# A decoder step on one core: the normalised h gets a buffer of its own before the split u is remade

## The reference, cut to what matters

```python
def _rms(x, g):
    x32 = x.astype(jnp.float32)
    y = x32 * lax.rsqrt(jnp.mean(x32 * x32, axis=-1, keepdims=True) + RMS_EPS)
    return (y * g.astype(jnp.float32)).astype(x.dtype)

def _half_ffn(h, g_pre, g_post, w_gate, w_up, w_down):
    u = _rms(h, g_pre)
    f = (jax.nn.silu(u @ w_gate) * (u @ w_up)) @ w_down
    return h + 0.5 * _rms(f, g_post)
...
        hp = _half_ffn(hp, *ffn1)
        qa, ka, va, qb, kb, vb, ga, gb = _split_in(_rms(hp, g_mix_pre[layer]), w_in[layer])
        oa, ob, bufs, pages = _prompt_mixer(qa, ka, va, qb, kb, vb, b_sb[layer])
        hp = _merge(hp, oa, ob, ga, gb, *out_w)
        hp = _half_ffn(hp, *ffn2)
```

## Time and profile before

| | |
|---|---|
| median of 3 runs | 1298.46 us (1297.64 to 1300.94) |
| the profiled execution, its own time | 1299.87 us |
| its span, first to last instruction | 1298.1 us |
| TensorE matmul busy | 1248.8 us, 96% |
| VectorE, ScalarE, GpSimd busy | 504.9, 409.7, 505.4 us |
| mean granted TensorE clock | 0.986 of full speed |

### The profile page before, as it was taken

The page is one execution under the profiler, slowest core; times in us unless marked ns, Lnnn a source line. Parts: engine busy times, 40 slices in busy tenths (PEclk is TensorE's granted clock), DMA queues, the critical chain, the costliest instruction groups (busy, mean ns, idle before and its releaser), DMA issues.

```text
span 1298.1 us, 24918 instructions
## 1 busy us (share of the span) xinstructions
PE 1248.8 (96%) x10504; PEld 1214.1 (94%) x10504; DVE 504.9 (39%) x921; ACT 409.7 (32%) x678; POOL 505.4 (39%) x415
## 2 busy tenths in 40 slices
PE   8989999999999999999999889999989999999996
PEld 7989999999998989999988779999989999999995
DVE  4572322321116450355467411838572322321115
ACT  6232222212224242344445322335232222212220
POOL 1334444444454334322322513372234444444441
PEclk9999999999999989999999989999989999999998
DMA  6122222222213223302221376131122222222211
GB/s 231 43 89 80 82 97 97 97 88 91 90 65 123 80 86 115 103 34 99 82 83 67 117 224 196 66 130 39 66 91 79 85 97 97 97 86 93 90 58 66
DMA packets 29075, 123.26 MB, mean 95 GB/s; under 512 B 4442, under 2 KB 10610, under 8 KB 17394
## 3 DMA queue, kind: packets, MB, share of 16 engines
q1 hardware_dynamic: 28994, 122.09, 27.1%
HBM read 115.39 MB, written 6.67 MB: 94 GB/s over the span
## 4 chain that ended last, share of the span: by engine, by line
PE 84%; DVE 8%; DVEq 2%; DMA 2%; ACT 2%; issue 1%; SPq 1%; POOL 1%; POOLq 0%; ACTq 0%
PE bank L1420 25%; PE bank L1421 25%; PE bank L1422 25%; DVEq L1056 2%; PE bank L1442 2%; DVE f L1082 1%; PE bank L1611 1%; DVE u_lo L1073 1%; PE bank L1668 1%; PE bank L1653 1%; PE bank L1691 1%; PE bank L1640 1%; PE bank L1677 1%; DVE rinv L1062 1%; POOL w_lo L578 1%
## 5 line engine op out<-in xcount | busy, mean ns | idle before, releaser
L578 POOL TENSOR_TENSOR w_lo<-raw,w_hi 128x512 fp32r<-128x512 f32 x368 | 477.2, 1329 | 753.3 <-ACT w_hi L653 567.1
L1420 PE MATMUL bank<-u_hi,w_hi 128*128 128x260 f32 x1952 | 564.8, 289 | 15.8 <-DVE u_lo L1073 10.5
L1421 PE MATMUL bank<-u_lo,w_hi 128*128 128x260 f32 x1952 | 554.8, 284 | 0.0
L1422 PE MATMUL bank<-u_hi,w_lo 128*128 128x260 f32 x1952 | 554.7, 284 | 0.0
L1420 PEld LDWEIGHTS bank<-u_hi,w_hi 128*128 128x128 f32 x1952 | 371.2, 190 | 29.1 <-issue 17.1
L1421 PEld LDWEIGHTS bank<-u_lo,w_hi 128*128 128x128 f32 x1952 | 371.8, 190 | 0.0
L1422 PEld LDWEIGHTS bank<-u_hi,w_lo 128*128 128x128 f32 x1952 | 371.6, 190 | 0.0
L653 ACT ACTIVATE w_hi<-raw 128x2048 fp32r<-128x2048 f32 x81 | 154.8, 1911 | 304.4 <-PE bank L1422 304.4
L1420 PE MATMUL bank<-hid_hi,w_hi 128*128 128x260 f32 x704 | 199.4, 283 | 1.0 <-POOL w_lo L578 1.0
L1421 PE MATMUL bank<-hid_lo,w_hi 128*128 128x260 f32 x704 | 198.9, 283 | 0.0
L1422 PE MATMUL bank<-hid_hi,w_lo 128*128 128x260 f32 x704 | 198.8, 282 | 0.0
(11 more groups left out here) (192 smaller groups left out, 1304.7 us busy)
## 6 DMA issues: line engine op xcount, KB each, us to landing
raw<-w_stream SPq DMA_DIRECT2D x84, 1024.0 KB, 4.8
raw<-w_stream SPq DMA_DIRECT2D x8, 768.0 KB, 4.3
e_raw<-w_stream SPq DMA_DIRECT2D x5, 1024.0 KB, 8.6
h<-x_t SPq DMA_DIRECT2D x4, 520.0 KB, 7.1
y_t<-h SPq DMA_DIRECT2D x8, 260.0 KB, 2.3
block<-kb_pool SPq DMA_DIRECT2D x8, 256.0 KB, 3.5
ring<-kb_pool SPq DMA_DIRECT2D x8, 256.0 KB, 3.1
ring<-vb_pool SPq DMA_DIRECT2D x8, 256.0 KB, 4.7
```

What stands on the lines that cost most here:

```text
L578: return pool.tensor_tensor(low[:, a], src[:, a], top[:, a].bitcast(F32), ALU.subtract)
L1420: pe.matmul(out, w, hi_x, start=first, stop=False)
L1421: pe.matmul(out, w, lo_x, start=False, stop=False)
L1422: return pe.matmul(out, v, hi_x, start=False, stop=last)
```

## The change

Three buffers hn of the size of h are added, in memory that is free at the time: hn[0] and hn[2] where the FFN's low hidden values come later, hn[1] where the values of the mixer's attention come later. VectorE writes h times rinv there (normed) during chunk 2, behind that group's items of chunk 2, and not after chunk 3. The remaking proper keeps the rounding and the low part. The wait for the old u to be used up passes from VectorE to ScalarE. On ScalarE the high part of chunk 5 comes behind the u_hi of both groups, and on VectorE one more item (up_scale of bank 1) comes ahead of the first group's low parts. The drains between the steps are gone.

```diff
+    hn = [Placed(nc, R + (0 if q == 1 else 74880))(f"hn{q}", [P, KD, T]) for q in range(3)]
...
-            def u_top_again(q, g):
+            def u_top_again(q, g, r):
+
+                act.wait_ge(hn_made, 8 * q + 4 * g + 4)
+                act.wait_ge(full[2 * g + 1], r)
                 for t in range(KD):
-                    if t % 2 == 0:
-                        act.wait_ge(hn_made, 8 * q + 4 * g + t // 2 + 1)
-                    act.activation(u_hi[:, t, tg(g)], f[:, t, tg(g)], ACT.Copy,
+                    act.activation(u_hi[:, t, tg(g)], hn[q][:, t, tg(g)], ACT.Copy,
                                    scale=gain[:, 2 * q, t:t + 1]).then_inc(uh_made, 1)
...
-                for c in range(2):
-                    hi(n0 + FOLD + c)
-                    u_top_again(q, c)
+                hi(n0 + FOLD)
+                for g in range(G):
+                    u_top_again(q, g, r0 + FOLD)
+                hi(n0 + FOLD + 1)
...
-                    dve.scalar_tensor_tensor(u_lo[:, t, at], (f if again else h)[:, t, at],
+                    dve.scalar_tensor_tensor(u_lo[:, t, at], (hn[q] if again else h)[:, t, at],
...
-            def u_again(q, g, r):
-
-                dve.wait_ge(full[2 * g + 1], r)
+            def normed(q, g):
                 for s in range(4):
                     part = (slice(None), slice(2 * s, 2 * s + 2), tg(g))
-                    dve.tensor_tensor(f[part], h[part], wide(g), ALU.mult).then_inc(hn_made, 1)
-                    if s:
-                        drain()
-                        u_low(q, g, s - 1, again=1)
-                drain()
-                u_low(q, g, 3, again=1)
+                    dve.tensor_tensor(hn[q][part], h[part], wide(g), ALU.mult).then_inc(hn_made, 1)
+
+            def u_again(q, g):
+                for s in range(4):
+                    u_low(q, g, s, again=1)
...
-                for b in range(4):
-                    gate_scale(1, b, r0)
+                for g in range(G):
+                    gate_scale(1, 2 * g, r0)
+                    gate_scale(1, 2 * g + 1, r0)
+                    normed(q, g)
                 up_scale(1, 0, r0)
                 up_gate(q, 1, 0)
-                u_again(q, 0, r0 + FOLD)
-                for b in range(1, 4):
+                up_scale(1, 1, r0)
+                u_again(q, 0)
+                for b in range(2, 4):
                     up_scale(1, b, r0)
-                u_again(q, 1, r0 + FOLD)
+                u_again(q, 1)
```

More of the change, by code:

```diff
@@ L901, in hi_part @@
                     split.then_inc(hi_made, 1)
-            for c in range(2):
-                hi(QKV + FOLD + c)
-                u_top_again(1, c)
+            hi(QKV + FOLD)
+            for g in range(G):
+                u_top_again(1, g, R_QKV + FOLD)
+            hi(QKV + FOLD + 1)
             for c in range(FOLD, 9):
@@ L1223, in _ @@
                     project_scale(c, 2 * g + 1)
-            for b in range(4):
-                project_scale(2, b)
+            for g in range(G):
+                project_scale(2, 2 * g)
+                project_scale(2, 2 * g + 1)
+                normed(1, g)
             project_scale(3, 0)
             project_scale(3, 1)
-            u_again(1, 0, R_QKV + FOLD)
+            u_again(1, 0)
             project_scale(3, 2)
             project_scale(3, 3)
-            u_again(1, 1, R_QKV + FOLD)
+            u_again(1, 1)
             def place_v(n):
```

## The result

| | before | changed |
|---|---|---|
| median | 1299.41 us (4 runs; 1298.46 of the 3 shown ahead) | 1279.22 us (1278.53 to 1281.35, 4 runs) |
| ratio, 95% interval | | 0.9849 [0.9835, 0.9864] |
| the profiled execution, its own time | 1299.87 us | 1279.07 us |
| span | 1298.1 us | 1277.1 us |
| TensorE matmul busy | 1248.8 us | 1237.4 us |

The kernel is 1.5% faster, 19.6 us (17.7 to 21.4); 19.3 were forecast.

What follows compares the result with a forecast made beforehand. TensorE, busy 96% of the span, bounds the kernel; time goes where it stops or runs slowly. Three remakings lose 22.9 us, less two new stops of 1.8: 19.3 gained, 1298.46 - 19.3 = 1279.2 us, range 1275 to 1286.

Steps and rivals of the forecast that it cites:

- The size of the loss: Bank 0 of chunk 3 to bank 0 of chunk 5: three remakings lose 8.2 + 8.2 + 6.5 = 22.9 us.
- the two new stops: TensorE before chunk 5, one in each FFN: 1.8 us each, taken off the 22.9 us gained.
- The multiplications for nothing in chunk 2: VectorE in chunk 2: four multiplications of 0.69 us per group fit into idle time, cost zero.
- 5.5 us a place: Multiplications in chunk 2: what they would cost at each place without the cover of VectorE's idle time.
- Second group on time: First FFN: the second group's low parts end at 69.7 us, TensorE wants the first at 71.4; the old stop goes.
- The longer stop: TensorE before chunk 5 in each FFN, behind chunk 3's hidden values: about 1.8 us instead of 0.82, bounds 0 and 2.9.
- 69.7 + 0.5 = 70.2: First FFN: VectorE's start on chunk 3's hidden values, about 70.2 us, after the second group's low parts end at 69.7.
- Rival 2: Before chunk 5 in the FFNs: VectorE stands through all four GpSimd instructions, 2.9 us a stop, 1281.4 us; chance 0.08.
- The low part of chunk 5: GpSimd in the first FFN: ready at 76.4 to 77.0 us, wanted at 77.2; just hidden, cost 0 (0 to 0.5).
- The rival of the clock: New stop before chunk 5 in the FFNs: the clock still falls there, 1.7 us each, 1282.6 us; chance 0.10.
- rival 3: The rival of the clock by its number: clock falls at the new stop, 1.7 us each, 1282.6 us; chance 0.10.
- rivals 4 and 6: FFNs before chunk 5: 4, nine stretched hidden-value instructions, 1291 us, chance 0.06; 6, slower by VectorE-GpSimd conflict, 1306, chance 0.02.

Runs made afterwards that it cites:

- e5: The kernel before, with the product in a buffer of its own and the wait for the old u moved to ScalarE, all orders kept: 1299.08 us, ratio 0.9992.
- e7: The kernel before, with ScalarE's SiLU of each bank waiting only for the hidden values up to that bank: 1296.42 us, ratio 0.9977.
- e1: The changed kernel, with the multiplications put back right before their group's low parts, behind the items of chunk 3: 1301.01 us, ratio 1.0011.
- e3: The changed kernel, with ScalarE's SiLU of each bank waiting only for chunk 3's hidden values up to that bank, not all four: 1274.65 us, ratio 0.9817.
- e4: The changed kernel, with GpSimd waiting for all hidden values of chunk 3 before the low part of chunk 5, both FFNs: 1281.90 us, ratio 0.9866.
- e2: The changed kernel with ScalarE's old order, the high part of chunk 5 between the u_hi of the two groups: 1284.04 us, ratio 0.9896.

## Why the prediction was right

*The size of the loss.* 22.9 us were read from the distances between chunk 3 and chunk 5. The change gave back 6.8, 6.8 and 6.5 in them, 20.1 of the 20.8 us between the two profiled executions. TensorE's waits for u_lo alone would have given 10.5. One reservation: the projection's 29.5 is from one execution; e5 and e7, which leave TensorE the same wait there, have 28.6. The difference is in the clock: from 473 to 481 us it is 0.57 on the mean in the profile of before, 0.79 in that of e5. So 0.9 us of the 22.9 belongs to that execution.

*The agreement.* That the median came out at 1279.22, forecast 1279.2, is in part luck. The median of before rose by 0.95 us with its fourth run, and the gain is 20.2 us by the medians, 19.6 by the ratio. In the sum the loss was 0.9 us too large and the two new stops together 0.8 us too large, which cancel.

*The multiplications for nothing in chunk 2.* Right, at 0.63 instead of 0.69 us; the delay of the first item of chunk 3 was nil in the FFNs and 0.1 in the projection. That the loss of the cover would cost "5.5 us a place" was too low: with ScalarE's new order it cost 8.1, 5.6 and 8.3 (e1).

*Second group on time.* Ready at 69.3, wanted from 71.2 on; forecast 69.7 and 71.4, in an execution that runs 0.3 us earlier.

*The longer stop.* Forecast 1.8 us a place, measured 24.4 - 23.0 = 1.4. (The forecast's own terms, 78.9 - 77.2, give 1.7.) Its mechanism is shown from both sides by e3 and e4. The size was off by the term "69.7 + 0.5 = 70.2": VectorE began the hidden values 4.0 us after the end of chunk 3, not 4.5. The gap of 0.5 us between the last low part and the first hidden value was misread; 78.26 + 1.87 = 80.13 and the next start at 80.22 give 0.09, and so does the changed kernel (66.01 + 3.31 = 69.32, then 69.41). The nine instructions themselves took 7.9, forecast 8.0; three were through before GpSimd started, not two, four were stretched as forecast, and two were clear of it. Rival 2 (GpSimd first each time) is out: four stretched instructions, not one of 5.5 us. Its upper bound was added up wrongly: 71.0 + 5.5 + 7 x 0.47 + 0.7 - 77.2 is 3.3 us, not 2.9, and its time 1282.2 instead of 1281.4, still inside the range.

*The low part of chunk 5.* Ready at 76.1 and wanted at 76.9; in e3, where it alone could stop TensorE, it did not.

*The rival of the clock.* It did not fall at this stop of 1.16 us (1.00 in the windows from 71 to 81). But in e4 it fell after one of 1.81, in both FFNs, and what the windows there lack of full clock adds up to 1.7 us each, the price that rival 3 had (and the clock's share in rivals 4 and 6): 0.43 x 4, from the clock of 0.57 over the 4 us from 77 to 81 in the earlier trace rows. So the mechanism of rival 3 exists, and the row of 1.60 us without a fall was a thin ground against it.

*What was missed.* ScalarE's order was costed at nothing, as a delay that fits into slack. It is a gain of 5 to 6 us (e2): the high part of chunk 5 behind both groups holds GpSimd back from VectorE until the low parts of u are written, and the second group is rounded sooner. Counted from bank 0 of chunk 3, the hidden values start 5.6 us later in e2 than in the changed kernel: the second group's low parts begin 1.8 us later and take 3.8 us longer. In the sum this did not show, because the second group was worked out with GpSimd's new start; taken part by part, the forecast would have credited all to the multiplications. The early products without the order keep 70 to 75% of the gain (e2), the order without the early products nothing (e1).

## What to carry to other kernels

Measure a loss between two points of the critical engine's steady pace, not by adding its waits: here the waits for u_lo showed 10.5 of 22.9 us, and the rest was slow clock (0.57 for 4 us in the first FFN), the stop before chunk 5 (0.82 us there) and hand-over (in the changed kernel a stop of 1.16 us made the stretch 1.4 longer). When two engines slow each other down, as VectorE (7.12 us against 3.31) and GpSimd (5.46 against 4.99) do here, an order on a third that delays one of them can be worth several us though no work is removed (5 to 6 us here), so look at what a moved instruction releases. A buffer that only removes a wait gives nothing where the waiting engine comes late anyway (ratio 0.9992 in e5); it pays when it lets work move into idle time. After each step ask which wait for "all of them" could be one for "the ones up to here".

## What the runs showed of the hardware

- In e4 the clock fell to 0.50 of full speed after a stop of 1.81 us ended by GpSimd, and stayed there for 3.4 us: in the first FFN 1.4 us after TensorE had resumed at 78.37, in the second 0.7 us after it had resumed at 942.71. After the stops of 1.16 to 1.59 us in the FFNs of the changed kernel it did not fall. Windows of TensorE (busy us, instructions; PEclk; DMA; GB/s) around it:

```profile
77.00:78.00 1.00, 0.00 (x0) 1.00 0.00 0
78.00:79.00 1.00, 0.63 (x5) 1.00 0.00 0
79.00:80.00 1.00, 1.00 (x11) 0.91 0.58 74
80.00:81.00 1.00, 1.00 (x6) 0.50 0.80 319
```

  and in the second FFN:

```profile
943.00:944.00 1.00, 1.00 (x8) 0.70 0.53 74
944.00:945.00 1.00, 1.00 (x7) 0.50 0.61 197
```

  So the first matmuls behind the stop still ran at full pace, and those at half the clock came after them. In the first FFN each of those first ones is recorded with 0.28 us while the next starts 0.12 us after it, from 78.60 to 79.68, so the distance of the starts tells the pace; from 79.98 on it is 0.22 us, with 0.42 recorded. How long that takes differs between the two FFNs, 1.4 and 0.7 us.
- Beside each other VectorE and GpSimd both take longer: GpSimd's four instructions take 5.46 us beside VectorE (changed kernel) and 4.99 alone (e4); eight low parts on VectorE take 7.12 beside GpSimd (e2) and 3.31 alone (changed kernel).
